# A decoder step with 32 routed experts on one core: part of the early expert weights issued later, the stage barrier ahead of the first list load, the overflow order and the first output sum placed otherwise

## What is computed

```python
proj = x @ w_in
ya = gdn_mixer(proj, ...)            # convolution, gated delta rule with state, 4 heads of 128
yb = pool_mixer(proj[..., COL_P:], ...)   # moving means over 2, 4, 8, 16 tokens
mix = concatenate([ya, yb]) @ w_out
h = layer_norm(ALPHA * x + mix, ln1_g, ln1_b)
# hier_moe: each token picks one of 4 groups, then 2 of its 8 experts (1024 -> 2x256 -> 1024)
y = layer_norm(ALPHA * h + hier_moe(h), ln2_g, ln2_b)
```

## Time and profile before

| | us |
|---|---|
| median of 3 runs (lowest, highest) | 1095.74 (1094.08, 1096.2) |
| the profiled execution | 1095.24 |
| its span, first to last instruction | 1093.5 |
| mean granted TensorE clock | 0.939 |
| TensorE busy / VectorE / ScalarE / GpSimd | 964.7 / 427.7 / 177.1 / 231.9 |
| DMA moved, mean | 186.53 MB, 171 GB/s |

### The profile page before, as it was taken

The page is one execution under the profiler, slowest core; times in us unless marked ns, Lnnn a source line. Parts: engine busy times, 40 slices in busy tenths (PEclk is TensorE's granted clock), DMA queues, the critical chain, the costliest instruction groups (busy, mean ns, idle before and its releaser), DMA issues. The chain is left out here.

```text
span 1093.5 us, 13478 instructions
## 1 busy us (share of the span) xinstructions
PE 964.7 (88%) x5387; PEld 541.6 (50%) x5387; DVE 427.7 (39%) x972; ACT 177.1 (16%) x378; POOL 231.9 (21%) x235
## 2 busy tenths in 40 slices
PE   6999999999997979999999986059899999999692
PEld 4666666655555746776667654023333333333141
DVE  0433343558304345766677745131111111111066
ACT  0222142211013101110111100011111111111012
POOL 0011011121005312134333222112111111210157
PEclk9999999999997779999999996569999999999887
DMA  6111011031426322031114225717779999999674
GB/s 257 39 39 39 20 39 39 20 78 39 132 83 206 127 65 70 14 122 49 49 39 164 78 96 211 297 33 295 302 290 395 412 421 400 415 387 369 255 287 151
DMA packets 61181, 186.53 MB, mean 171 GB/s; under 512 B 22952, under 2 KB 36296, under 8 KB 51560
## 3 DMA queue, kind: packets, MB, share of 16 engines
q1 hardware_dynamic: 34320, 157.20, 37.5%
q0 software_dynamic: 8240, 19.09, 4.7%
q10 hardware_dynamic: 18560, 9.38, 3.0%
HBM read 164.76 MB, written 30.01 MB: 178 GB/s over the span
## 5 line engine op out<-in xcount | busy, mean ns | idle before, releaser
L369 PE MATMUL pj<-xT,wblk 128*128 128x384 f32 (+1 forms) x960 | 299.0, 473 | 14.5 <-DMA xT<-in_xt_dram 8.4
L369 PEld LDWEIGHTS pj<-xT,wblk 128*128 128x128 f32 x960 | 182.7, 192 | 125.6 <-issue 16.1
L1829 PE MATMUL e<-space,xgT 128*32 128x512 f32 x1056 | 170.9, 595 | 5.9 <-issue 3.2
L1146 PE MATMUL b<-space 128*128 128x512 f32 x288 | 133.8, 608 | 0.5 <-DVE xt L1486 0.5
L1829 PE MATMUL e<-space,acT 128*32 128x512 f32 x576 | 86.8, 592 | 0.7 <-ACT acT L1907 0.7
L1829 PE MATMUL e<-szT,acT 128*32 128x512 f32 x192 | 86.3, 592 | 0.0
L1146 PEld LDWEIGHTS b<-space 128*128 128x128 f32 x288 | 52.9, 194 | 56.5 <-issue 55.4
L1829 PEld LDWEIGHTS e<-space,xgT 128*32 128x32 f32 x1056 | 46.3, 110 | 66.1 <-issue 64.4
L1952 DVE SCALAR_TENSOR_TENSOR ac<-sg,lst,e 128x256 f32<-128x256 f32 x24 | 11.5, 480 | 170.5 <-ACT sg L1903 170.5
L1829 PE MATMUL e<-qkvT,xgT 128*32 128x512 f32 x480 | 72.0, 603 | 0.0
L1767 POOL DMA_INDIRECT picked_dram<-yo,lst x24 | 23.7, 988 | 216.1 <-PE e L1813 169.8
(11 more groups left out here) (329 smaller groups left out, 1154.5 us busy)
## 6 DMA issues: line engine op xcount, KB each, us to landing
space<-in_w_gate_up_dram SPq DMA_DIRECT2D x22, 2048.0 KB, 19.3
space<-in_w_down_dram SPq DMA_DIRECT2D x24, 1024.0 KB, 11.6
qkvT<-in_w_gate_up_dram SPq DMA_DIRECT2D x11, 2048.0 KB, 12.2
wblk<-in_wcol_dram SPq DMA_DIRECT2D x20, 512.0 KB, 3.4
szT<-in_w_down_dram SPq DMA_DIRECT2D x8, 1024.0 KB, 16.9
space<-picked_dram SPq DMA_DIRECT2D x8, 1024.0 KB, 5.4
qkvT<-h_dram SPq DMA_DIRECT2D x9, 512.0 KB, 11.0
space<-in_w_out_dram SPq DMA_DIRECT2D x1, 4096.0 KB, 22.0
```

The costliest lines, as they stand in the source:

```text
L369: last = pe.matmul(pj[par][:, bank * 512:bank * 512 + m], wblk[par][:, k, :], xT[:, k, a:a + m], start=(k == 0), stop=(k == KT - 1))
L1146: last = pe.matmul(b[6 + half][:, :], src[:, kk, :], wout[:, k, half * 512:(half + 1) * 512], start=(k == H), stop=(k == H - 1))
L1829: last = pe.matmul(out[at, :], lhsT[:, at], theirs if j == GROUP - 1 else mine, start=start, stop=stop)
```

## The change

Four edits.

1. `load_list(0)` and the gathers of passes 0 and 1 leave `c2`: ScalarE waits for the scatters and issues all eight lists at the start of `c4`; GpSimd waits for list 0 there and issues the two gathers ahead of its small load.
2. `overflow_order` is run by VectorE at the end of `c2`, after `place(LAST)`, in tiles that `c2` has already (`sq`, `xt`); `order_ready` is kept.
3. Of the eight weight loads that SyncE issues at `r == LAST`, five (8 MB) are issued in `c4`, ahead of the overflow work of SyncE, once gather 1 has landed, in another order: own down 2, own gate/up 3, shared gate/up 1, shared down 1, own gate/up 4.
4. In `c5` TensorE leaves out tile 0; VectorE adds its two rows in SBUF and goes on from there. The waits of the reloads and the counts of `summed[0]` follow.

```diff
@@ c2, SyncE, r == LAST
                             load_own_dn(0)
                             load_own_dn(1)
-                            load_own_gu(3)
-                            load_own_dn(2)
-                            load_own_gu(4)
-                            load_shared_gu(1)
-                            load_shared_dn(1)
@@ c2, GpSimd, end
                     scatter(LAST)
                     e.wait_ge(xg_cleared, 2)
-                    e.wait_ge(h_out, 16 * LAST)
-                    e.wait_ge(h_last, 16)
-                    e.wait_ge(lst0_in, 32)
-                    for q in range(2):
-                        gather_rows(q)
@@ c2, ScalarE, end
                     weigh(LAST)
-                    e.wait_ge(listed, 16 * 2 * NT)
-                    load_list(0, lst0_in)
                     e.wait_ge(h_last, 16)
@@ c2, VectorE, end
                     place(LAST)
+                    overflow_order(e)
@@ c4, SyncE, start
+                    e.wait_ge(gathered[1], 16)
+                    load_own_dn(2)
+                    load_own_gu(3)
+                    load_shared_gu(1)
+                    load_shared_dn(1)
+                    load_own_gu(4)
                     overflow(e, body)
@@ c4, GpSimd, start
+                    e.wait_ge(lst_in[0], 32)
+                    for q in range(2):
+                        gather_rows(q)
                     pool.dma_start(olst[:, :], tab_d[NE * SLOTS:NE * SLOTS + P, :]).then_inc(ov_free, 16)
                     gather(2)
@@ c4, ScalarE, start
-                    for g in range(1, NE // GROUP):
+                    e.wait_ge(listed, 16 * 2 * NT)
+                    for g in range(NE // GROUP):
                         load_list(g, lst_in[g])
@@ c4, VectorE, start
-                    overflow_order(e)
                     x_turned_v(e, 0, 0)
@@ c5, SyncE
                     for n in range(NB, NT):
-                        e.wait_ge(summed[n % NB], n // NB)
+                        if n == NB:
+                            e.wait_ge(ysum_read[0], 1)
+                        else:
+                            e.wait_ge(summed[n % NB], n // NB - (n % NB == 0))
@@ c5, TensorE, step
+                        if isinstance(i, int) and i == k == 0:
+                            return
@@ c5, VectorE, front
-                        e.wait_ge(summed[k], i + 1)
+                        total = ysum[k][:, :]
+                        if isinstance(i, int) and i == k == 0:
+                            e.wait_ge(in_ready[0], 16)
+                            total = picked[0][:, 0:D]
+                            dve.tensor_tensor(total, total, picked[0][:, D:], ALU.add).then_inc(first, 1)
+                            e.wait_ge(first, 1)
+                        else:
+                            e.wait_ge(summed[k], i if k == 0 else i + 1)
...
-                        dve.scalar_tensor_tensor(out=r, in0=done(i, k), scalar=ALPHA, in1=ysum[k][:, :],
+                        dve.scalar_tensor_tensor(out=r, in0=done(i, k), scalar=ALPHA, in1=total,
```

More of the change, by code:

```diff
@@ L844, in build @@
         kept = phase(whole)
-        lst0_in, gathered = kept("lst0_in"), [kept(f"gathered{k}") for k in range(2)]
+        listed, order_ready = kept("listed"), kept("order_ready")
+        gathered = [kept(f"gathered{k}") for k in range(2)]
         in_ready, ln2_in = [kept(f"in_ready{k}") for k in range(NB)], kept("ln2_in")
@@ L943, in build @@
             kqs = yaT
+            flat_sq = sq[:, :, :].rearrange("p a d -> p (a d)")
+            nov, cuma, cumb = (flat_sq[:, k * NE:(k + 1) * NE] for k in range(3))
+            ove, ovs = (flat_sq[:, 3 * NE + k * MAXOV:3 * NE + (k + 1) * MAXOV] for k in range(2))
+            cmpm = xt[:, 0:MAXOV * NE].rearrange("p (o n) -> p o n", n=NE)
             b = [pb(f"b{i}", [P, 512], c2) for i in range(8)]
@@ L977, in build @@
                                                                              "ex_ready"))
-            both_ready, fixed, slot_ready, listed = S("both_ready"), S("fixed"), S("slot_ready"), S("listed")
+            both_ready, fixed, slot_ready, ochain = S("both_ready"), S("fixed"), S("slot_ready"), S("ochain")
             cleared2, xg_cleared, h_last = S("cleared2"), S("xg_cleared"), S("h_last")
@@ L1675, in build @@
             carried, hres_in = S("carried"), S("hres_in")
-            ochain, order_ready = S("ochain"), S("order_ready")
             wgu_o = gu_of(rows_of[:, 0:GU])
@@ L1682, in build @@
             acT_o = gates_of[:, ND * DN:ND * DN + FE].rearrange("p (c t) -> p c t", t=P)
-            nov, cuma, cumb = (sb(n, [P, NE], ctx=c4) for n in ("nov", "cuma", "cumb"))
-            cmpm = sb("cmpm", [P, MAXOV, NE], ctx=c4)
-            ove, ovs = sb("ove", [P, MAXOV], ctx=c4), sb("ovs", [P, MAXOV], ctx=c4)
-            lst_in = [lst0_in] + [S(f"lst_in{g}") for g in range(1, NE // GROUP)]
+            lst_in = [S(f"lst_in{g}") for g in range(NE // GROUP)]
             scattered = S2("scattered")
@@ L2036, in build @@
             S2 = lambda n: [S(f"{n}{i}") for i in pr]
-            chn = S("chn2")
+            chn, first = S("chn2"), S("first")
             summed, ysum_read, var_ready, rstd1, rstd_ready, norm_ready, g_ready, out_ready, stored = (
```

62 lines of the change are left out of this document (31 added, 31 removed).

## The result

The changed kernel took 1081.45 us in the median of 4 runs (1078.1 to 1083.82), beside 1095.97 for the kernel before (1094.08 to 1097.81): ratio 0.9858, 95% interval 0.9822 to 0.9894, so 1.1 to 1.8% faster. The forecast was 1083.0. The profiled execution took 1080.91 us, its span was 1079.1 (before 1093.5) and the mean granted clock 0.941 (before 0.939).

What follows compares the result with a forecast made beforehand. TensorE was taken to bound the kernel nearly everywhere, with holes at the mixer-to-expert and last-stage handovers. 11.7 - 0.6 + 1.6 = 12.7 off the profiled 1095.24 gives 1082.5, plus 0.5 for the median: 1083.0, range 1079.5 to 1088.5.

Steps and rivals of the forecast that it cites:

- Part 1: Mixer-to-expert handover: barrier ahead of the list load and order chain moved bring the first product from 725.16 to 713.4, gaining 11.7 us.
- Who is last at the barrier: End of the mixer's block: GpSimd's drain done at 697.0 to 698.0, VectorE's order chain last at 699.03, by 1.0 us.
- Stage and list: Start of the expert stage: release 699.1 plus 1.8 gives 700.9; list issue to gather 3.7 us, gather 0 at 704.6.
- Gather and turns: Start of the expert stage: gather lands in 4.3 us, TensorE turns at 708.9, first product at 713.4 without the 7.93 wait.
- the two bounds on it: Clock at the first expert products: up at once wins 1.3 us more; as late as in the last stage loses about 0.7.
- The scatter beside the chain: End of the mixer's block: rival, last scatter held until VectorE's chain is done, 7.3 us later, gain 5.4, 1090.3; chance 0.05.
- Part 2: Expert stage: 8 of 12 MB issued behind the second gather; no wait for weights, gather 2 late, 0.6 us lost.
- The slower rival: Expert stage: gather 2 starves until the 8 MB are through, landing near 737; 2.9 us slower, 1098.6; chance 0.03.
- list and gather slow: Start of the expert stage: list pair takes 4.4, first gathers 12.9; part 1 shrinks by 2.0 + 8.6, 1093.6; chance 0.04.
- The transfer rival: Expert passes: transfers bound them, the 3 us backlog returns as waits; gain 9, 1087; chance 0.12.
- Part 3: Last stage: VectorE adds tile 0, TensorE starts with tile 1, done at 1047.9 against 1049.51; 1.6 us gained.
- The sum: Whole kernel: 11.7 - 0.6 + 1.6 = 12.7 us gained.

Runs made afterwards that it cites:

- chain_late: The changed kernel with the overflow order chain back at the start of the expert stage; 1078.37 us, ratio 0.9849 to the kernel before.
- defer_alone: The kernel before with only the five weight loads (8 MB) moved behind gather 1 in the expert stage; 1100.79 us, ratio 1.0063.
- wait_removed: The changed kernel with SyncE's five deferred weight loads issued without the wait for gather 1; 1095.27 us, ratio 1.0002 to the kernel before.
- all_in: two_sums plus the edit of drain_free and four unread constant products on TensorE at the start of the last stage; 1075.43 us, ratio 0.9796.
- weights_early: The changed kernel with all eight weight loads (12 MB) issued in the mixer's stage as before; 1082.91 us, ratio 0.9906 to the kernel before.
- drain_free: The changed kernel without GpSimd's own wait for its last two scatters at the end of the expert stage; one execution, 1084.68 us.
- two_sums: The changed kernel with list 0 before the barrier, order chain split, weights behind all lists, VectorE adding last-stage tiles 0 and 1; 1077.59 us, ratio 0.9840.

## Why the prediction was right

**The reading of the bound** held: one hole between mixer and experts, and a small one before the last stage. TensorE's busy work is untouched.

**Part 1, first product.** Forecast at 713.4 by the clock of the trace, found at 713.34. That is partly luck: the last cast came 0.95 later than in the trace before. From the cast's start, the forecast was 23.7 (713.4 - 689.72) and 22.7 was found, so the gain was 12.77 where the sum had 11.7.
- *Who is last at the barrier.* The forecast had GpSimd's drain done at 697.0 to 698.0 and VectorE at 699.03, last by 1.0. Found: the drain began at 692.13 and lasted 3.94, to 696.07; VectorE's chain ended at 699.87. VectorE was last, but by 3.8, and this is the term that was mis-sized: 4.1 to 5.1 was added behind the end of the last scatter, where 2.2 was found (696.07 - 693.90). The forecast counted from where GpSimd's own part ended, but in both traces the drain, put on the queue shortly ahead of the last indirect DMA's record, ended 1.0 to 1.1 after that DMA had landed: before, the gather of 705.55 landed in 5.0, at 710.6, and the drain ended at 711.6; after, the scatter of 692.93 landed in 2.1, at 695.0. The mis-size changed nothing in the sum, since VectorE was last either way, but it hid that edit 2 has a price: chain_late showed 3.7.
- *Stage and list.* The list was issued 10.56 from the cast, where 11.2 was forecast (700.9 - 689.72): release and clear took 1.35 (699.87 to 701.22) instead of 1.8. List to gather took 3.2, where 3.7 was put. These two are the 1.1 by which the handover was better. What the weights did to the small transfers is larger than the reading of the list pair alone: the last scatter took 6.5 to land before and 2.1 after, and the first list load waits for it.
- *Gather and turns.* 4.23 to the turn, forecast 4.3; turn to product 4.72, forecast 4.5. The 7.93 us wait of the earlier trace rows is gone. The clock came up as late as before: 0.50 to 716, and the first products at half rate for 2.57 us in both traces, so neither of the two bounds on it was drawn.
- *The scatter beside the chain* (rival). The last two scatters ran 0.99 and 0.97 us with VectorE's chain beside them (the second beside fp32 copies of 0.15 to 0.43 us), against 0.97 of the earlier trace rows with VectorE idle, and the stage opened at 701, not 708. The rule of the Trainium skill, SBUF — State Buffer, "SBUF: two separate sides", is that a two-port operation of VectorE keeps GpSimd from writing descriptors for the whole of that instruction. That is not the whole chain: a hold until VectorE is done, which the rival priced at 7.3 us, doesn't follow from it. This trace shows no loss beside such short copies; what long ones would do no run here shows.

**Part 2.** Gather 2 was issued at 711.39 (forecast 711.65) and landed 11.1 later, at 722.5; it was wanted at 723.15. So 0 was lost where 0.6 was put; the margin was 0.65 us. Later gathers of line 861 landed in 4.2/13.1/14.9 (least, median, most), as in the earlier trace rows. The timeline of GpSimd's and TensorE's part of it:

```profile
711.39 1.03 POOL L861 DMA_INDIRECT xg<-h_dram,lst  x1 [4.01 <-PE e L1847]
...
723.15 1.04 PE L1847 MATMUL e<-cst,xg 128*128 128x128 f32 x8
```

The 8 MB were in at 737.4, forecast 735, well ahead of pass 3 (746.6 by the same spacing). The slower rival, a gather that gets nothing until the weights are through, fell: 11.1 us against the 26 that the weights took. The Trainium skill, DMA: Bandwidth & Descriptors, "Queues, rings and completion order", says that a DMA engine takes the queues it has work for in turn, a packet at a time; by that the gather can't wait for all 8 MB, and the trace agrees. The text costed ScalarE's list issues at nothing, because they "end some 7 us after 700.9". They ended at 709.25, 1.4 ahead of ScalarE's first copy and 2.1 ahead of the weights, and so it held; defer_alone (held issues) and wait_removed (a late list 0) show what lies on the other side of that margin. No rival of the forecast names it: "list and gather slow" had the right place and 10.6 us for it, but not the condition, which is that the weights are issued while lists still are.

**The transfer rival** didn't show: first product to last scatter 305.37 before, 305.32 after. TensorE's three waits at passes 17, 20 and 23 (turn to turn, less the 11.68 us of a pass) sum to 4.98 before and 4.9 after, and to 4.4 to 8.6 in the other kernels; that is the noise under which 2 us differences disappear, and the granted clock makes the larger part of it (see all_in).

**Part 3.** Forecast: tile 1's load 10.76 after the last scatter (1041.3 - 1030.54); found 10.68 (1029.35 - 1018.67). Tile 1 then took 5.8 and not 6.64, since the clock came up within it: 0.62 in 1032 to 1034 (the window shown with the result), 3 to 5 us after TensorE's first product at 1029.39. Before, it was at 0.67 only in 1044 to 1046, 5 to 7 us after the first product at 1039.44:

```profile
1044.00:1046.00 2.00, 2.00 (x5) 0.83 (x4) 0.00 (x0) 0.00 (x0) 0.00 (x0) 0.67 0.00 0
```

Why it rose sooner against that product than before is open. So 2.47 instead of 1.6, and 0.9 of it is this part. It varies: over the kernels in which VectorE adds tile 0 alone, tile 1 came 15.96 to 17.54 after the last scatter, against 18.52 to 19.03 where TensorE adds it, so the forecast's 1.6 and the 2.47 both lie within what the edit gives.

**The sum** was 12.7 and 14.3 was found in the spans: +1.1 in the handover, +0.6 at the gather, +0.9 in the last stage, -0.95 by the last cast.

## What to carry to other kernels

A weight load that is deferred must be ordered behind every small load that still has to be *issued*, not only behind the one that is wanted first: with 8 MB in the queues some small list loads of this kernel held their issuing engine 4 to 9 us at a time, the first one landed up to 13 us late, and one wait decided between 1.5% faster and nothing. Before a long chain is moved to another stage, look for the transfer that could cover it where it stands: here the list load and the gather did, and by the traces the move cost 3.7 us of the gain. An edit's share holds only beside the others: the deferral was worth 1.5 us in one order of the stages and 7.5 in the other. And count the parts from marks inside the trace when the work ahead of them varies by more than the term under test.

## What the runs showed of the hardware

- The issue of a small list load took 0.33 to 0.8 us without bulk loads beside it. Beside 8 MB of weights that another engine's queue had issued, three issues of defer_alone took 3.82, 6.08 and 6.86 us and two of wait_removed 9.16 and 7.39. The issuing engine was held for that time: in defer_alone ScalarE's first copy came 13.5 us behind VectorE's.
- Small transfers landed late beside large ones: list scatters in 6.2 to 6.6 us beside 12 MB and in 2.1 without, the DMAs of list 0 in 8.9 and 15.3 beside 8 MB and in 1.8 and 2.0 without.
- GpSimd's drain behind indirect transfers varied: 7.11 us before at the end of c2, 3.94 in the changed kernel there, 6.67 in defer_alone, 8.38 in weights_early, 4.07 to 4.23 at the end of c4 though all scatters had landed by then, 5.54 in drain_free. In the first four it ended 1.0 to 1.2 us after the last transfer landed; in drain_free some 2.1 after. What rule it follows was not settled.
- Filling TensorE's wait with four unread products had the granted clock at 1.00 for its first real tile (all_in), where it was 0.50 for most of that tile without them (two_sums). VectorE then had a tile every 4.2 us from the start.
- Waits of 2 to 3 us in the expert passes were followed by a granted clock of 0.50 in some traces (all_in, defer_behind_lists, two_sums) and by 1.00 in others (before, 2.60 us). A place of that kind cost 3.7 to 6.0 us in the former and at most 2.7 where the clock stayed up.
